# A mixture-of-experts stage that gathers its rows with two interleaved streams of indirect DMAs instead of blocks of eight

## The chip, the core and the metric

The kernel runs on one core of a Trainium2 chip. A core has five engines with instruction streams of their own: PE (matrix products), DVE (vector work), ACT (activation functions, copies), POOL (general work; here it also begins the gathers) and SP (begins plain DMAs). They meet through semaphores only. Sixteen DMA engines carry out the transfers that the engines begin. The metric is the device time of one launch in microseconds (us); 2831.47 us is the median of three runs of the kernel before.

## What is computed

Two layers of a hybrid decoder trunk, for 256 prompt tokens and 64 sample tokens together (320 tokens in three tiles of 128, 128 and 64). In each layer two recurrences are followed by a "PEER" mixer and by a gated per-layer embedding. The change lies in the PEER mixer, in which every token takes, for each of 8 heads, the 16 best of 16,384 experts, each a row `u` and a row `v` of 1,024 floats:

```python
sv, si = lax.top_k(s, PEER_TOPK)
cand = sv[:, :, 0, :, None] + sv[:, :, 1, None, :]
cv, ci = lax.top_k(cand.reshape(...), PEER_TOPK)
idx = jnp.take_along_axis(cand_idx.reshape(...), ci, axis=-1)
gate = jax.nn.softmax(cv, axis=-1)
u = jnp.take(u_tab, idx, axis=0)
hid = jax.nn.gelu(jnp.einsum('td,thkd->thk', xb, u).astype(jnp.float32), approximate=False)
vv = jnp.take(v_tab, idx, axis=0)
return jnp.einsum('thk,thkd->td', (gate * hid).astype(xb.dtype), vv)
```

Every sum over `k` needs all of `u` and `v` from HBM: 16 x 2 rows of 4 KB a token and head.

## The kernel before, in words

The mixer of a layer is a loop of 20 steps (NSTEP): 8 heads for the first tile of tokens, 8 for the second, 4 for the sample tile (which holds its 64 tokens twice, so two heads go in one step). A step has two halves of eight experts (G = 8). One gather brings one expert's row for each of 128 tokens, 128 rows of 4 KB, into one slot of a ring of eight: `urow` for U and `vrow` for V, both in the large tile `arena` (so the profile calls them arena). A layer has 320 U and 320 V gathers. The engines share a step as follows:

- POOL begins the gathers (`gather_step`, U at L671, V at L677), in one order written in its loop. Ahead of a U gather it waits for `u_free`, which DVE raises when its dot product has used the row eight before; ahead of a V gather for `v_free`, which PE raises when it has used the V row eight before. At the start of a step it also waits for `idx_ready`, the expert numbers of the step.
- DVE (`dots`, L1179) forms the product of each landed U row with the tokens, eight to a half. After the first half of a step it picks the experts of the next step (`pick_experts`, L1108 to L1170), a chain of some 25 small instructions. After the second half comes, in some steps, part of the embedding (`embed`, L1203 and L1205).
- ACT (`weights`) takes gelu of the eight products (L1003) and, after DVE has multiplied by the gates, makes eight diagonal matrices of the weights (L1009), which need all eight products of the half.
- PE (`add_rows`) multiplies each diagonal matrix with its V row and sums in PSUM. Between the halves of steps 0 to 7 it forms the queries and scores of heads to come (`between`), with weights that SP loads.

The embedding of a finished tile of tokens is worked into later steps, by the table `behind`: tile 0 is normed after step 8, and its four column blocks (i, m) = (0, 0) to (0, 3) come after the second halves of steps 9, 10, 11 and 12; tile 1 is normed in step 16, its blocks come two after step 16 and two after step 17. In each of them PE does its matrix products after its `add_rows` of that half (L1997 to L2003 and behind), ACT takes a sigmoid (L1034), and DVE waits for that sigmoid (L1203), adds the result to `h`, and only then goes on to the dots of the next step. Tile 2 is done at the end.

Of the kernel before, what the change touches and what calls it, by code (L numbers as in the profile page):

```python
# [33 lines left out]
TOPK = 16  # L34
G = 8
# [5 lines left out]
def hybrid_trunk(nc, x_prompt, x_sample, state_gla, state_gdn, state_conv, p_prompt, p_sample,  # L41
# [28 lines left out]
    NSTEP = sum(STEPS)  # L70
# [12 lines left out]
    with ctx:  # L83
        def sb(name, shape, dt=F32):
            return ctx.enter_context(nc.sbuf_tensor(name, shape, dt))
# [40 lines left out]
        idx_u = sb("idx_u", [P, 2, TOPK], U32)  # L126
# [22 lines left out]
        def view(off, *dims, rows=P):  # L149
            n = 1  # L150
            for d in dims:
                n *= d
            assert off + n <= ARENA, (off, dims)
            v = arena[0:rows, off:off + n]
            if len(dims) == 2:
                v = v.rearrange("p (a b) -> p a b", b=dims[1])
            elif len(dims) == 3:
                v = v.rearrange("p (a b c) -> p a b c", b=dims[1], c=dims[2])
            return v
# [77 lines left out]
        urow = view(0, G, D)  # L237
        vrow = view(G * D, G, D)
# [57 lines left out]
        def lsem(name):  # L296
            layer_sems.append(sem(name))
            return layer_sems[-1]
# [111 lines left out]
        idx_ready = lsem("idx_ready")  # L410
        u_loaded = [lsem(f"u_loaded{r}") for r in range(G)]
        v_loaded = [lsem(f"v_loaded{r}") for r in range(G)]
        u_free = lsem("u_free")
        v_free = lsem("v_free")
# [120 lines left out]
        def _(pool):  # L535
# [41 lines left out]
            with pool.Fori(0, DEPTH) as layer:  # L577
# [81 lines left out]
                u_l = peer_u.rearrange("l e d -> (l e) d")  # L659
                v_l = peer_v.rearrange("l e d -> (l e) d")  # L660

                def gather_step(step):

                        par_ = step % 2
                        pool.wait_ge(idx_ready, step + 1)
                        for half in range(2):
                            done = step * TOPK + half * G
                            for r in range(G):
                                at = idx_u[:, par_, half * G + r:half * G + r + 1]
                                pool.wait_ge(u_free, done + r + 1)  # L670
                                pool.indirect_dma_start(  # L671
                                    urow[:, r, :], None, u_l,
                                    bass.IndirectOffsetOnAxis(ap=at, axis=0)).then_inc(u_loaded[r], 16)
                            for r in range(G):
                                at = idx_u[:, par_, half * G + r:half * G + r + 1]
                                pool.wait_ge(v_free, done + r + 1)
                                pool.indirect_dma_start(  # L677
                                    vrow[:, r, :], None, v_l,
                                    bass.IndirectOffsetOnAxis(ap=at, axis=0)).then_inc(v_loaded[r], 16)

                for step in range(NSTEP):
                    gather_step(step)

                pool.wait_ge(u_free, G + NSTEP * TOPK)
                pool.wait_ge(v_free, G + NSTEP * TOPK)
# [30 lines left out]
        def _(act):  # L716
# [46 lines left out]
            with act.Fori(0, DEPTH) as layer:  # L763
# [135 lines left out]
                for k, (to, _, _, who) in enumerate(solve):  # L899
                    for i in solve_tiles(k):  # L900
                        n += 1
                        if who == "act":
                            R = ROWS[i]
                            act.wait_ge(solve_mm, n)
                            act.activation(slot(to[i], R)[:, :, 0:R], heads(i + 3 * (k % 2), R, R),
                                           ACT.Copy).then_inc(solve_act, 1)
# [153 lines left out]
        def _(dve):  # L1060
# [146 lines left out]
            with dve.Fori(0, DEPTH) as layer:  # L1207
# [215 lines left out]
                for k, (to, _, _, who) in enumerate(solve):  # L1423
                    for i in solve_tiles(k):
                        n += 1
                        R = ROWS[i]
                        src, t = heads(i + 3 * (k % 2), R, R), slot(to[i], R)[:, :, 0:R]
                        if who == "act":
                            continue
                        dve.wait_ge(solve_mm, n)  # L1430
                        if k == N_T:
                            own.after(dve.scalar_tensor_tensor(
                                slot(SH[i])[:, :, :], src, -1.0, over_heads(ident, R), ALU.mult,
                                ALU.add))
                        if who == "+":
                            dve.tensor_tensor(t, src, t, ALU.add).then_inc(solve_dve, 1)
                        else:
                            dve.tensor_copy(t, src).then_inc(solve_dve, 1)
# [633 lines left out]
```

## Time and profile before

| | us |
|---|---|
| three runs | 2816.63, 2837.72, 2831.47 (median 2831.47) |
| the profiled execution's own time | 2820.99 |
| its span | 2819.5 |
| PE / DVE / POOL busy in the span | 2185.9 / 1435.8 / 1548.5 |
| first dot to last dot of the mixer, layer 1 | 366.1 to 1357.9 |
| first dot to last dot of the mixer, layer 2 | 1761.0 to 2757.9 |

The two mixers take about 1,990 of the 2,820 us. The profile tells for each engine what it did when, and for an idle stretch what ended it. A gather shows twice: as an instruction of POOL, which is the time that POOL takes to begin it, and in the DMA share, which is how busy the sixteen DMA engines were. It has landed some time after POOL's instruction ended. "<-issue" behind an idle time says that the engine waited for nothing that the profile shows; "<-remote" that a semaphore ended the wait whose writer the profile doesn't name.

### The profile page before, as it was taken

What the parts mean: (1) busy time and instruction counts of PE and PEld (TensorE: products, weight loads), DVE (VectorE), ACT (ScalarE), POOL (GpSimd) and SP (SyncE); (2) the same over time, 40 slices, a digit from 0 to 9 for tenths busy, and PEclk for the clock granted to TensorE, in tenths of its full rate; (3) what the DMA queues carried; (4) which work ended last, traced back from release to release, by engine and by line L of the source; (5) the groups of instructions that cost most, each with busy time, mean ns of one, the idle gap of its engine ahead of it and who ended that gap; (6) DMA issues with size and microseconds to landing.
All of it is one profiled execution on the core that took longest, in us unless ns stands there. A gap on an engine that the chain in (4) does not pass through costs nothing.

```text
span 2819.5 us, 22006 instructions
## 1 busy us (share of the span) xinstructions
PE 2185.9 (78%) x6992; PEld 1231.9 (44%) x6992; DVE 1435.8 (51%) x3577; ACT 655.5 (23%) x1520; POOL 1548.5 (55%) x1385
## 2 busy tenths in 40 slices
PE   7999888877858576767799888898886667764775
PEld 5658654433323232334366676544432233332343
DVE  1446355565654565555224553565665556566452
ACT  3232222221221121221231431221221212112212
POOL 1113076777766677766210131767676766777661
PEclk9988999998878788889899999999987887897897
DMA  6310299999998889988463104999999988899783
GB/s 189 120 58 8 79 347 361 365 383 381 353 358 314 296 308 341 359 289 320 161 183 113 50 5 144 368 359 386 356 384 360 327 303 309 302 366 344 279 322 124
DMA packets 258740, 759.32 MB, mean 269 GB/s; under 512 B 26908, under 2 KB 89300, under 8 KB 258620
## 3 DMA queue, kind: packets, MB, share of 16 engines
q0 software_dynamic: 188480, 686.97, 65.7%
q1 hardware_dynamic: 70140, 70.88, 7.8%
q8 instruction: 60, 0.98, 0.1%
q14 instruction: 60, 0.49, 0.1%
HBM read 749.04 MB, written 8.72 MB: 269 GB/s over the span
## 4 chain that ended last, share of the span: by engine, by line
PE 40%; DVE 18%; issue 14%; POOL 12%; another core or an unknown queue 7%; ACT 5%; DMA 4%; SPq 0%; DVEq 0%; ACTq 0%; POOLq 0%; PEldq 0%
PE ps L1519 39%; DVE arena L1179 9%; POOL arena L671 6%; POOL arena L677 6%; DMA arena<-in_peer_u_dram,idx_u 2%; DMA arena<-in_peer_v_dram,idx_u 1%; ACT arena L1009 1%; DMA wring<-in_w_peer_q_dram 1%; ACT L1003 1%; DVE pick L1159 0%; DVE arena L1149 0%; DVE ci L1141 0%; PE ps L1535 0%; DVE arena L1155 0%
## 5 line engine op out<-in xcount | busy, mean ns | idle before, releaser
L1519 PE MATMUL ps<-arena 128*128 128x512 f32 (+5 forms) x3736 | 1427.3, 542 | 510.1 <-ACT arena L1009 386.1
L1519 PEld LDWEIGHTS ps<-arena 128*128 128x128 f32 (+3 forms) x3736 | 675.5, 206 | 1243.1 <-issue 1202.0
L677 POOL DMA_INDIRECT arena<-in_peer_v_dram,idx_u x640 | 755.2, 1180 | 313.2 <-issue 179.3
L671 POOL DMA_INDIRECT arena<-in_peer_u_dram,idx_u x640 | 687.8, 1075 | 335.2 <-issue 190.7
L1179 DVE CUSTOM_DVE_ANT_0 arena<-arena,xn 128x1024 f32<-128x1024 f32 x640 | 755.4, 1221 | 224.3 <-DMA arena<-in_peer_u_dram,idx_u 199.4
L1519 PE MATMUL ps<-aT,wring 128*128 128x320 f32 (+2 forms) x1344 | 362.9, 430 | 20.7 <-DMA wring<-in_w_peer_q_dram 11.2
L1519 PEld LDWEIGHTS ps<-aT,wring 128*128 128x128 f32 x1344 | 253.3, 196 | 129.7 <-issue 25.9
L1519 PE MATMUL ps<-wring,aT 128*128 128x256 f32 (+1 forms) x960 | 222.7, 388 | 5.8 <-ACT aT L1024 4.5
L1519 PEld LDWEIGHTS ps<-wring,aT 128*128 128x128 f32 (+1 forms) x960 | 177.3, 189 | 52.3 <-issue 20.8
L1203 DVE TENSOR_TENSOR arena<-arena,ps 128x256 f32<-128x256 f32 x24 | 10.1, 421 | 336.9 <-ACT arena L1034 336.9
L1003 ACT ACTIVATE gelu<-hid 128x8 f32<-128x8 f32 x80 | 16.6, 208 | 642.7 <-DVE hid L1179 440.0
L1009 ACT ACTIVATE arena<-ident,wgt 128x128 f32<-128x128 f32 x512 | 157.0, 388 | 20.8 <-DVE wgt L1185 11.5
L598 POOL TENSOR_TENSOR arena<-arena 128x1024 f32<-128x1024 f32 x4 | 12.3, 3106 | 216.1 <-PE ps L1519 109.9
L1185 DVE TENSOR_TENSOR wgt<-gelu,gate 128x8 f32<-128x8 f32 x80 | 13.4, 168 | 183.9 <-ACT gelu L1003 114.0
L1034 ACT ACTIVATE arena<-ps 128x256 f32<-128x256 f32 x24 | 9.2, 384 | 279.9 <-remote 185.0
L1003 ACT ACT_TABLE_LOAD x54 | 69.3, 1283 | 0.9
L588 POOL TENSOR_TENSOR arena<-xn,seqmask 64x1024 f32<-64x1024 f32 x8 | 16.1, 2033 | 94.0 <-ACT xn L789 94.0
L973 ACT ACTIVATE arena<-ps 128x320 f32<-128x320 f32 (+1 forms) x32 | 13.6, 424 | 228.5 <-PE ps L1519 212.5
L982 ACT ACTIVATE arena<-ps 128x256 f32<-128x256 f32 x30 | 10.0, 381 | 212.9 <-PE ps L1519 97.4
L933 ACT ACT_TABLE_LOAD x40 | 51.3, 1283 | 4.8 <-issue 4.1
L1179 DVE DVE_READ_ACCUMULATOR2_ANT hid<- 128x1 f32 x640 | 52.0, 81 | 0.0
L639 POOL TENSOR_TENSOR arena<-arena,seqmask 64x1024 f32<-64x1024 f32 x8 | 14.9, 1890 | 62.3 <-ACT arena L915 62.3
(293 smaller groups left out, 1460.6 us busy)
## 6 DMA issues: line engine op xcount, KB each, us to landing
wring<-in_w_in_dram SPq DMA_DIRECT2D x28, 1024.0 KB
wring<-in_w_peer_q_dram SPq DMA_DIRECT2D x16, 1024.0 KB
arena<-in_peer_u_dram,idx_u POOLq DMA_INDIRECT x640
arena<-in_peer_v_dram,idx_u POOLq DMA_INDIRECT x640
wring<-in_w_out_dram SPq DMA_DIRECT2D x8, 1024.0 KB
wring<-in_w_ple_gate_dram SPq DMA_DIRECT2D x8, 1024.0 KB
arena<-in_state_gdn_dram POOLq DMA_DIRECT2D x2, 2048.0 KB, 15.4
out_dram<-arena POOLq DMA_DIRECT2D x2, 2048.0 KB, 11.7
```

Of the source, the lines that this page charges most:

```text
L588: ins = pool.tensor_tensor(vmask[:, hd, :, :], v1[0:64, 2, hd * P:(hd + 1) * P].unsqueeze(1).to_broadcast([64, NB, P]), seqmask[:, :].unsq ...
L598: ins = pool.tensor_tensor(s_, s_, d.to_broadcast([P, NB, P]), ALU.mult)
L639: ins = pool.tensor_tensor(dvm[hd], vnew(2, 64)[:, hd, :].unsqueeze(1).to_broadcast([64, NB, P]), seqmask[:, :].unsqueeze(2).to_broadcast( ...
L671: pool.indirect_dma_start(urow[:, r, :], None, u_l, bass.IndirectOffsetOnAxis(ap=at, axis=0)).then_inc(u_loaded[r], 16)
L677: pool.indirect_dma_start(vrow[:, r, :], None, v_l, bass.IndirectOffsetOnAxis(ap=at, axis=0)).then_inc(v_loaded[r], 16)
L933: act.activation(gexp[:, :], cv[:, :], ACT.Exp, bias=ncv[:, 0:1], accum_out=esum[:, 0:1]).then_inc(gate_exp, 1)
L973: act.activation(qT[:, c, t0:NT], ps[:, 6 + c, t0:NT], ACT.Copy)
L1003: act.activation(gelu[:, par_, c], hid[:, par_, c], ACT.Gelu).then_inc(gelu_ready, 1)
L1009: act.activation(diag[:, r, :], unit[:, :], ACT.Copy, scale=wgt[:, par_, k:k + 1]).then_inc(diag_ready, 1)
L1179: dve.tensor_tensor_reduce(out=urow[:, r, :], in0=urow[:, r, :], in1=xn[:, tile, :], scale=1.0, scalar=0.0, op0=ALU.mult, op1=ALU.add, acc ...
L1185: dve.tensor_tensor(wgt[:, par_, c], gelu[:, par_, c], gate[:, par_, c], ALU.mult).then_inc(wgt_ready, 1)
L1519: return pe.matmul(out, lhsT, rhs, start=start, stop=stop, skip_group_check=True)
```

## The change

In the old loop POOL begins the gathers of a half as eight U and then eight V, then the next half. In the new one a counter k runs over all U rows of the layer; at each k the U gather of row k is begun, and then the V gather of row k - 8. So the V rows of a half are begun one by one between the U rows of the half after it. The waits ahead of each gather keep their semaphores and counts, and the wait for `idx_ready` stands ahead of the first U row of a step. DVE, ACT, PE and SP keep their orders, instruction for instruction.

```diff
                 u_l = peer_u.rearrange("l e d -> (l e) d")
                 v_l = peer_v.rearrange("l e d -> (l e) d")
 
-                def gather_step(step):
-
-                        par_ = step % 2
+                def gather_u(k):
+                    step, c, r = k // TOPK, k % TOPK, k % G
+                    if c == 0:
                         pool.wait_ge(idx_ready, step + 1)
-                        for half in range(2):
-                            done = step * TOPK + half * G
-                            for r in range(G):
-                                at = idx_u[:, par_, half * G + r:half * G + r + 1]
-                                pool.wait_ge(u_free, done + r + 1)
-                                pool.indirect_dma_start(
-                                    urow[:, r, :], None, u_l,
-                                    bass.IndirectOffsetOnAxis(ap=at, axis=0)).then_inc(u_loaded[r], 16)
-                            for r in range(G):
-                                at = idx_u[:, par_, half * G + r:half * G + r + 1]
-                                pool.wait_ge(v_free, done + r + 1)
-                                pool.indirect_dma_start(
-                                    vrow[:, r, :], None, v_l,
-                                    bass.IndirectOffsetOnAxis(ap=at, axis=0)).then_inc(v_loaded[r], 16)
-
-                for step in range(NSTEP):
-                    gather_step(step)
+                    at = idx_u[:, step % 2, c:c + 1]
+                    pool.wait_ge(u_free, k + 1)
+                    pool.indirect_dma_start(
+                        urow[:, r, :], None, u_l,
+                        bass.IndirectOffsetOnAxis(ap=at, axis=0)).then_inc(u_loaded[r], 16)
+
+                def gather_v(k):
+                    step, c, r = k // TOPK, k % TOPK, k % G
+                    at = idx_u[:, step % 2, c:c + 1]
+                    pool.wait_ge(v_free, k + 1)
+                    pool.indirect_dma_start(
+                        vrow[:, r, :], None, v_l,
+                        bass.IndirectOffsetOnAxis(ap=at, axis=0)).then_inc(v_loaded[r], 16)
+
+                for k in range(NSTEP * TOPK + G):
+                    if k < NSTEP * TOPK:
+                        gather_u(k)
+                    if k >= G:
+                        gather_v(k - G)
 
                 pool.wait_ge(u_free, G + NSTEP * TOPK)
                 pool.wait_ge(v_free, G + NSTEP * TOPK)
```

POOL's order at the start of a layer's mixer, before. L671 is a U gather and L677 a V gather, x8 means eight in a row, and the waits are in brackets; the last two rows begin the second step:

```order
L671 DMA arena<-in_peer_u_dram,idx_u 128x1024 [waits u_free] x7
L677 DMA arena<-in_peer_v_dram,idx_u 128x1024 [waits v_free] x8
L671 DMA arena<-in_peer_u_dram,idx_u 128x1024 [waits u_free] x8
L677 DMA arena<-in_peer_v_dram,idx_u 128x1024 [waits v_free] x8
L671 DMA arena<-in_peer_u_dram,idx_u 128x1024 [waits u_free,idx_ready]
L671 DMA arena<-in_peer_u_dram,idx_u 128x1024 [waits u_free] x7
```

The same place now, up to the fourth V gather; L668 is U and L676 is V. The alternation goes on so through all 20 steps:

```order
L668 DMA arena<-in_peer_u_dram,idx_u 128x1024 [waits u_free] x8
L676 DMA arena<-in_peer_v_dram,idx_u 128x1024 [waits v_free]
L668 DMA arena<-in_peer_u_dram,idx_u 128x1024 [waits u_free]
L676 DMA arena<-in_peer_v_dram,idx_u 128x1024 [waits v_free]
L668 DMA arena<-in_peer_u_dram,idx_u 128x1024 [waits u_free]
L676 DMA arena<-in_peer_v_dram,idx_u 128x1024 [waits v_free]
```

The ninth U gather, which needs the first dot, has moved ahead of the first V gather; before, all eight V gathers stood ahead of it.

The end of a layer's mixer on POOL, before:

```order
L671 DMA arena<-in_peer_u_dram,idx_u 128x1024 x8
L677 DMA arena<-in_peer_v_dram,idx_u 128x1024 x8
L671 DMA arena<-in_peer_u_dram,idx_u 128x1024 x8
L677 DMA arena<-in_peer_v_dram,idx_u 128x1024 x8
```

and now:

```order
L668 DMA arena<-in_peer_u_dram,idx_u 128x1024
L676 DMA arena<-in_peer_v_dram,idx_u 128x1024
L668 DMA arena<-in_peer_u_dram,idx_u 128x1024
L676 DMA arena<-in_peer_v_dram,idx_u 128x1024
L668 DMA arena<-in_peer_u_dram,idx_u 128x1024
L676 DMA arena<-in_peer_v_dram,idx_u 128x1024 x9
```

Between the last eight U gathers there now stand V gathers of the half before, and nine V gathers close the layer instead of eight.

## Rows read from the trace of the kernel before

**Rows 1.** The page's costliest groups: line, engine, count | busy, mean ns | idle before.

```profile
L677 POOL DMA_INDIRECT arena<-in_peer_v_dram,idx_u x640 | 755.2, 1180 | 313.2 <-issue 179.3
L671 POOL DMA_INDIRECT arena<-in_peer_u_dram,idx_u x640 | 687.8, 1075 | 335.2 <-issue 190.7
...
L1203 DVE TENSOR_TENSOR arena<-arena,ps 128x256 f32<-128x256 f32 x24 | 10.1, 421 | 336.9 <-ACT arena L1034 336.9
```

**Rows 2.** Busy time by stretch: PE, PEld, DVE, ACT, POOL; PEclk, DMA share, GB/s.

```profile
366.00:753.00 387.00, 321.25 (x865) 163.92 (x866) 225.86 (x578) 84.47 (x234) 289.40 (x253) 0.92 0.97 369
753.00:868.00 115.00, 79.09 (x175) 35.44 (x173) 59.29 (x149) 24.77 (x60) 74.49 (x75) 0.81 0.93 355
868.00:1033.00 165.00, 113.08 (x258) 53.07 (x258) 85.85 (x225) 34.12 (x76) 114.55 (x96) 0.82 0.85 305
1033.00:1290.00 257.00, 177.15 (x416) 83.00 (x416) 145.30 (x372) 52.57 (x131) 180.57 (x160) 0.83 0.89 327
2265.00:2428.00 163.00, 112.45 (x258) 52.94 (x258) 85.16 (x222) 33.38 (x76) 113.06 (x96) 0.82 0.86 309
2428.00:2690.00 262.00, 174.63 (x416) 82.34 (x416) 146.10 (x374) 53.33 (x131) 180.60 (x160) 0.84 0.88 321
```

**Rows 3.** Timeline of POOL in step 12: start, us, instruction, idle time before it.

```profile
983.96 1.99 POOL L671 DMA_INDIRECT arena<-in_peer_u_dram,idx_u  x1 [0.31 <-issue]
...
993.52 0.94 POOL L677 DMA_INDIRECT arena<-in_peer_v_dram,idx_u  x1 [0.30 <-issue]
...
1007.61 0.94 POOL L677 DMA_INDIRECT arena<-in_peer_v_dram,idx_u  x1 [0.30 <-issue]
1008.85 0.94 POOL L671 DMA_INDIRECT arena<-in_peer_u_dram,idx_u  x1 [0.30 <-issue]
...
1027.54 0.94 POOL L677 DMA_INDIRECT arena<-in_peer_v_dram,idx_u  x1 [0.30 <-issue]
```

**Rows 4.** Timeline of PE, ACT and DVE in step 12 and after it.

```profile
1007.51 15.67 PE L1519 MATMUL ps<-arena 128*128 128x512 f32 x32 [2.30 <-ACT arena L1009]
1023.02 1.03 PE L1519 MATMUL ps<-arena,pT 128*128 128x256 f32 x4
...
1024.60 3.72 PE L1519 MATMUL ps<-wring,aT 128*128 128x256 f32 x16
...
987.47 0.21 ACT L1003 ACTIVATE gelu<-hid 128x8 f32<-128x8 f32 x1 [8.81 <-DVE hid L1179]
...
1006.53 0.21 ACT L1003 ACTIVATE gelu<-hid 128x8 f32<-128x8 f32 x1 [10.98 <-DVE hid L1179]
...
1031.78 0.38 ACT L1034 ACTIVATE arena<-ps 128x256 f32<-128x256 f32 x1 [21.07 <-remote]
...
1032.20 0.42 DVE L1203 TENSOR_TENSOR arena<-arena,ps 128x256 f32<-128x256 f32 x1 [25.26 <-ACT arena L1034]
...
1033.00 1.22 DVE L1179 CUSTOM_DVE_ANT_0 arena<-arena,xn 128x1024 f32<-128x1024 f32 x1
...
1034.14 1.22 DVE L1179 CUSTOM_DVE_ANT_0 arena<-arena,xn 128x1024 f32<-128x1024 f32 x1
```

**Rows 5.** POOL's waits over the span: us in total, times, longest.

```profile
POOL arena L671 <- DVE hid L1179: 82.9, 12, 11.8
POOL arena L677 <- PE ps L1519: 82.5, 89, 5.4
```

**Rows 6.** Timeline of PE in steps 3 and 4: where two adds begin.

```profile
512.35 17.00 PE L1519 MATMUL ps<-arena 128*128 128x512 f32 x44 [2.89 <-ACT arena L1009]
...
556.93 17.01 PE L1519 MATMUL ps<-arena 128*128 128x512 f32 x44 [2.89 <-ACT arena L1009]
```

**Rows 7.** The chain that ended last: a gather on it, start and us.

```profile
1163.22 6.24 DMA arena<-in_peer_u_dram,idx_u
```

**Rows 8.** Timeline of POOL at the end of the second mixer.

```profile
2764.05 0.94 POOL L677 DMA_INDIRECT arena<-in_peer_v_dram,idx_u  x1 [0.30 <-issue]
```

**Rows 9.** Timeline of DVE in the pick of step 14.

```profile
1092.94 0.43 DVE L1138 MAX8 cv<-arena 128x8 f32<-128x256 f32 x1 [5.34 <-issue]
```

## The prediction, made before the changed kernel ran

> **What bounds the kernel now.** I read the costliest groups of the page first. The two gather lines of Pool, 640 instructions each, are busy 755 and 688 us of the 2819.5 us, and one row shows a different loss: DVE stands idle 336.9 us ahead of only 24 instructions of L1203, the adding of the embedding [rows 1]. The busy table by stretch then cuts the first layer's mixer stage by steps: steps 0 to 7, 8 and 9, 10 to 12, 13 to 17 [rows 2]. In steps 0 to 7 Pool starts 253 gathers in 387 us, one in 1.53 us, with the DMA engines at a share of 0.97. In steps 10 to 12 it starts 96 in 165 us, 55 us a step, with the DMA share at 0.85; the second layer's stretch (163 us) repeats it. So there are two regimes.
>
> In the first, Pool's issue and the transfers run at about the same pace. A gather is busy 0.94 us and the next follows after 0.30 us, 1.24 us in all, while some take 1.99 us, and these stand where DVE runs its dots (1.22 us each, one every 1.14 us) [rows 3, 4]. The mean busy time in steps 0 to 7 is 289.40 / 253 = 1.144 us, so without any wait an issue would cost 1.144 + 0.30 = 1.444 us and a step of 32 issues 46.2 us [rows 2]. The rest up to 1.53 us is waiting: Pool waited 82.5 us ahead of V gathers until PE had used a row, and 82.9 us ahead of U gathers for dots [rows 5]. PE is close behind: its adding of V rows came round after 44.6 us (512.35 to 556.93) [rows 6].
>
> In the second regime, the steps that end with an embed, the chain is another. In step 12 the first V gather of the second half starts at 993.52, the last at 1007.61; then Pool runs on by itself and starts the next step's eight U and eight V gathers, 1008.85 to 1027.54, while DVE waits 25.26 us in L1203 [rows 3, 4]. That wait ends with PE's eight rows (15.67 us from 1007.51), PE's embed (1023.02 to 1024.60 + 3.72 = 1028.3), ACT's sigmoid at 1031.78 and DVE's add; the next dots start at 1033.00. So the second regime is a chain of DVE, PE and ACT, and half of Pool's issues lie beside it for nothing.
>
> **The change, part by part.** No gather is added or removed: 1,280 issues, 671 MB, the same two rings of eight rows. The waits are the same in number. What moves: U of a half now goes ahead of V of the half before, one by one. A U gather needs the dot of the row eight before it; the V gather behind it in Pool's order now waits with it. Before, the eight V gathers of the half stood ahead of these U gathers and could start while DVE was in its pick of experts or in an embed.
>
> *Steps with an embed (10 to 12).* While DVE waits in L1203 no dot ends, so Pool stands at the first U gather of the next half, and there is nothing to start: the V rows of the half that is waited for are the last that it may issue. The 16 issues at 1008.85 to 1027.54 that were free come into the chain. From a step's first dot to the next step's: dot 1.3; 31 issues ahead of the last V gather at 1.24 = 38.4; two bursts of dots, each with four issues of 1.99 instead of 0.94, 8 x 1.05 = 8.4; landing 6.0 (the chain shows 6.24 from issue to landing [rows 7]); the last row on PE 15.67 / 8 = 2.0; embed 5.3; sigmoid and two adds 0.38 + 0.42 + 0.42 = 1.2. Sum 62.6 against 55.0, so 3 x 7.6 = +23 us a layer. DVE's own work is covered: a burst of dots takes 8 x 1.14 = 9.2 us, and from one burst's gelu to the next's are 1006.53 - 987.47 = 19.1 us [rows 4], so the pick between them takes 9.9. Both end 19 us after the first dot, before Pool has issued the 16 gathers that come first, so Pool doesn't wait for the pick there. Bounds: four long issues instead of eight and a landing of 5 give 57.4; the lag between PE's end (1028.3) and the sigmoid (1031.78), which I leave out because the transfers will have run dry by then, gives 66.1 if it stays.
>
> The landing is the one term on which a page speaks. The Trainium skill, "DMA: Bandwidth & Descriptors", section "Anatomy of one DMA", fits 2.0 us + bytes / 436e3, an estimate of 3.2 us for 512 KB; the trace's 6.24 differs and decides. By the page each such cycle would be 2.8 us shorter, 22 us over the eight of both layers.
>
> *Steps 0 to 9.* From step 0's first dot to step 10's lie 387 + 115 = 502 us [rows 2]. In the new order Pool issues 20 halves of 16 in between; the last begins after 319 issues, and 1.3 + 6.0 + 2.0 + 5.3 + 1.2 = 15.8 us stand around them. At 1.444 us an issue that is 476 us, at the present 1.53 us 504 us. The V waits of eight-row blocks should shrink, since a V row is asked for some 22 us after its predecessor landed. But PE's and ACT's loop of 44.6 us, SP's weight blocks, and a new wait remain: U gathers need the first dot after a pick, which by 32 x 1.444 = 46 us a step comes only some 5 us before Pool's turn. I take 1.49 us: 491 us, -11.
>
> *Steps 13 to 17.* Before: 257 us, and 262 us in the second layer [rows 2]. New: step 13 starts with all rows landed; the last V gather of step 16 begins after 1.3 + 127 x 1.444 = 184.7; landing, row, two embeds (10.6) and the adds make 204.5; step 17 with its two embeds takes 62.6 + 5.3 = 67.9. Sum 272.4, +15, and +10 in the second layer; mean +12.5. Here the 16 gathers that were prefetched beside the embed are paid back, so no gain is counted for them.
>
> *Tail.* Step 18 of the second layer begins where the stretch from 2428 ends, at 2690, and the last V gather starts at 2764.05, 74 us later [rows 2, 8]. New: 1.3 + 55 x 1.444 = 80.7, +6.5.
>
> Sum a layer: -11 + 23 + 12.5 + 6.5 = +31; two layers +62. Against the profiled execution's 2820.99 us that is **2883 us**; the median of the three runs shown is 2831.47, 10 us above it, inside what the runs differ by, so I leave the sum there.
>
> **The rivals.** *Faster: the V waits go and nothing else counts.* Pool never waits in steps 0 to 9 (1.444 us, -26), the embed cycles cost their lower bound (+2.4 each: +7 for steps 10 to 12, and 272.4 - 10.4 = 262, +3 to +5 for 13 to 17), and the tail costs nothing: -26 + 7 + 4 = -15 a layer, 2791 us. For it speak the 82.5 us of V waits [rows 5]; against it, that all 32 issues of an embed step, at 1.24 us or more, now lie inside its chain. It decides when the mean issue falls below 1.45 us in steps 0 to 9. Chance 0.12.
>
> *Flat.* Steps 0 to 9 gain 20 us a layer and embeds cost half of my price: about 2830 us. Chance 0.25.
>
> *Worse: more issues meet a dot.* Dots now run one by one as U rows land, every two issues, instead of in bursts of eight; each may hold up the issue beside it. At present (1.144 - 0.94) / 1.05 x 32 = 6 of 32 issues are long [rows 2, 3]. If ten are, a step costs 4.2 us more, over the 28 steps without an embed +118: 3001 us. The same sign has a pick that stands idle between its steps, as 5.34 us ahead of one MAX8 in step 14 [rows 9], once it outlasts the 5 us of slack. Against: isolated dots meet at most one issue, and an overlap shorter than a burst needn't hold it. Chance 0.13.
> The Trainium skill, "SBUF — State Buffer", section "SBUF: two separate sides", gives that rival a rule: a DVE operation with two SBUF inputs and a GpSimd one that reads SBUF exclude each other for a whole instruction. The 1.99 us issues beside dots agree with it; no run here yet shows dots one by one.
>
> *Not what it says.* Pool has one instruction order, written in the loop, so the order itself can't fail to change.
>
> **How the numbers follow.** My forecast (2845 to 2945) has 0.50, flat 0.25, faster 0.12, worse 0.13. The bounds of the terms give 2807 (1.444 us, 57.4 us cycles) to 2965 (1.53 us, 66.1 us cycles); with the rivals' ends cut to two in ten the range is 2815 to 2960. A change of 1%, 28 us, is about what a measurement of this kernel can tell from none. Above 2849: most of the forecast and the worse rival, 0.62; within 1%: 0.26; below 2793: 0.12.
>
> **What would show it.** Right: the steps with an embed are about 62 us long, Pool's wait ahead of U gathers for dots grows from 83 us to some 150 or more, waits ahead of V for PE nearly vanish, and the DMA share falls below 0.8 in steps 10 to 12. The last V gather of a half starts some 14 us or less before DVE's next dots. Wrong: embed steps at 55 us or below, or steps 0 to 7 faster than 1.45 us an issue; then Pool's waits, not its issue, were the price. If the mean gather is busy over 1.25 us, the worse rival holds.

## The result, and the profile of the changed kernel

The changed kernel takes 3076.16 us (median of 4 runs, 3054.41 to 3080.42), the kernel before 2834.59 us in the same rounds: a ratio of 1.085, 95% interval 1.079 to 1.091. I had forecast 2883 us and a range up to 2960. The direction was right and the size was not: the loss is 242 us where I worked out 62. The profiled execution took 3072.53 us and its span is 3071.0 us, 251.5 more than before.

The costliest groups of the page after, which answer to [rows 1] (L668 is the U gather, L676 the V gather, L1205 the embed's add, L1181 the dots; columns as there):

```profile
L668 POOL DMA_INDIRECT arena<-in_peer_u_dram,idx_u x640 | 714.0, 1116 | 672.5 <-DVE hid L1181 425.6
L1181 DVE CUSTOM_DVE_ANT_0 arena<-arena,xn 128x1024 f32<-128x1024 f32 x640 | 755.7, 1223 | 387.0 <-DMA arena<-in_peer_u_dram,idx_u 377.9
L676 POOL DMA_INDIRECT arena<-in_peer_v_dram,idx_u x640 | 758.2, 1185 | 200.0 <-issue 166.4
L1205 DVE TENSOR_TENSOR arena<-arena,ps 128x256 f32<-128x256 f32 x24 | 10.1, 421 | 392.7 <-ACT arena L1036 392.7
```

Busy on the gathers is 714.0 + 758.2 = 1472 us against 1443 before, only 29 us more. What grew is the idle time ahead of U gathers, 335 to 673 us, and the releaser that ends most of it is now the dot of DVE. POOL's waits of after say the same, against [rows 5] (us in total, times, longest):

```profile
POOL arena L668 <- DVE hid L1181: 425.6, 35, 20.8
POOL arena L676 <- PE ps L1521: 33.0, 97, 3.7
```

So the waits for PE fell from 82.5 to 33.0 us, as the order promised, and those for dots rose from 82.9 to 425.6 us. Waiting changed places, and much more came than went.

Where in the program? Busy time by stretch in layer 1 of after: steps 0 to 9, 10 to 12, 13 to 17 (us, then PE, PEld, DVE, ACT, POOL, granted clock, DMA share, GB/s, as in [rows 2]):

```profile
364.00:934.00 570.00, 420.98 (x1038) 192.87 (x1038) 282.56 (x726) 109.11 (x294) 361.21 (x320) 0.92 0.84 315
934.00:1122.00 188.00, 115.63 (x258) 46.31 (x258) 86.48 (x225) 34.38 (x76) 112.95 (x96) 0.91 0.73 268
1122.00:1414.00 292.00, 190.34 (x416) 74.88 (x416) 145.41 (x372) 53.06 (x131) 183.17 (x160) 0.91 0.78 288
```

The DMA share fell in each (steps 0 to 7 had 0.97 before), and the granted clock of TensorE is 0.91 to 0.92 throughout, no lower than in any stretch of [rows 2], so the clock is no part of the loss. The differences by stage, from first dot to first dot, beside the terms of the sum:

| stretch | before, layer 1 / 2 | after, layer 1 / 2 | change | forecast |
|---|---|---|---|---|
| steps 0 to 9 | 502.3 / 504.3 | 570.3 / 562.3 | +68 / +58 | -11 |
| steps 10 to 12 | 164.5 / 163.3 | 187.4 / 187.9 | +23 / +25 | +23 |
| steps 13 to 17 | 257.3 / 261.5 | 292.1 / 286.4 | +35 / +25 | +15 / +10 |
| steps 18, 19, to the last dot | 66.5 / 66.6 | 76.9 / 75.2 | +10 / +9 | +6.5 (to the last V gather) |

Of the 190 us that the forecast missed, 148 lie in steps 0 to 9 (79 + 69). They are the question of the experiments.

The steps with an embed came as forecast. Timeline of POOL, then PE, ACT and DVE, in step 12 of after, whose first dot ran at 1058.77; it answers to [rows 3, 4]:

```profile
1106.98 0.94 POOL L676 DMA_INDIRECT arena<-in_peer_v_dram,idx_u  x1 [0.31 <-issue]
1123.38 1.69 POOL L668 DMA_INDIRECT arena<-in_peer_u_dram,idx_u  x1 [15.46 <-DVE hid L1181]
...
1113.51 1.98 PE L1521 MATMUL ps<-arena 128*128 128x512 f32 x4 [0.50 <-DMA arena<-in_peer_v_dram,idx_u]
...
1116.92 3.72 PE L1521 MATMUL ps<-wring,aT 128*128 128x256 f32 x16
...
1120.67 0.38 ACT L1036 ACTIVATE arena<-ps 128x256 f32<-128x256 f32 x1 [24.26 <-PE ps L1521]
...
1121.09 0.42 DVE L1205 TENSOR_TENSOR arena<-arena,ps 128x256 f32<-128x256 f32 x1 [28.45 <-ACT arena L1036]
...
1121.89 1.22 DVE L1181 CUSTOM_DVE_ANT_0 arena<-arena,xn 128x1024 f32<-128x1024 f32 x1
```

After its last V gather POOL does nothing for 15.46 us; PE gets that row, the embed follows, the sigmoid, the add, and only the next dot lets POOL go on. First dot to first dot is 63.1 us (forecast 62.6), the last V gather starts 48.2 us behind the first dot (48.1) and the next dots 14.9 us behind that (14.5). The sigmoid came 0.03 us after PE's end (1116.92 + 3.72), not 3.5 us as in [rows 4].

### The profile page after: what moved, and what is told of

Its sections match the earlier page's. It is cut to its first block, busy times and chain, and to the rows that moved or that the text cites. A ratio compares the mean times of both kernels' runs of the same rounds, so it can differ in the third digit from the quotient of the medians.

```text
span 3071.0 us, 22006 instructions
## 1 busy us (share of the span) xinstructions
PE 2262.7 (74%) x6992; PEld 1184.7 (39%) x6992; DVE 1432.3 (47%) x3577; ACT 656.1 (21%) x1520; POOL 1578.0 (51%) x1385
## 4 chain that ended last, share of the span: by engine, by line
PE 32%; POOL 23%; issue 13%; DVE 13%; DMA 12%; another core or an unknown queue 4%; ACT 3%; SPq 0%; DVEq 0%; ACTq 0%; POOLq 0%; PEldq 0%
PE ps L1521 31%; POOL arena L668 11%; POOL arena L676 11%; DMA arena<-in_peer_v_dram,idx_u 8%; DVE arena L1181 4%; DMA arena<-in_peer_u_dram,idx_u 2%; DMA wring<-in_w_peer_q_dram 1%; ACT arena L1011 0%; DVE cv L1140 0%; DVE pick L1161 0%; DVE arena L1151 0%; DVE arena L1157 0%; DVE topi L1130 0%; DVE arena L1119 0%
## 5 line engine op out<-in xcount | busy, mean ns | idle before, releaser
L1521 PE MATMUL ps<-arena 128*128 128x512 f32 (+5 forms) x3736 | 1506.5, 545 | 695.4 <-DMA arena<-in_peer_v_dram,idx_u 320.1
L1521 PEld LDWEIGHTS ps<-arena 128*128 128x128 f32 (+3 forms) x3736 | 629.3, 202 | 1553.5 <-issue 797.8
L668 POOL DMA_INDIRECT arena<-in_peer_u_dram,idx_u x640 | 714.0, 1116 | 672.5 <-DVE hid L1181 425.6
L1181 DVE CUSTOM_DVE_ANT_0 arena<-arena,xn 128x1024 f32<-128x1024 f32 x640 | 755.7, 1223 | 387.0 <-DMA arena<-in_peer_u_dram,idx_u 377.9
L676 POOL DMA_INDIRECT arena<-in_peer_v_dram,idx_u x640 | 758.2, 1185 | 200.0 <-issue 166.4
L1205 DVE TENSOR_TENSOR arena<-arena,ps 128x256 f32<-128x256 f32 x24 | 10.1, 421 | 392.7 <-ACT arena L1036 392.7
L598 POOL TENSOR_TENSOR arena<-arena 128x1024 f32<-128x1024 f32 x4 | 12.7, 3193 | 212.5 <-DVE arena L1330 212.5
L1187 DVE TENSOR_TENSOR wgt<-gelu,gate 128x8 f32<-128x8 f32 x80 | 13.5, 169 | 224.4 <-ACT gelu L1005 139.7
L984 ACT ACTIVATE arena<-ps 128x256 f32<-128x256 f32 x30 | 10.0, 381 | 292.2 <-remote 153.3
L1181 DVE DVE_READ_ACCUMULATOR2_ANT hid<- 128x1 f32 x640 | 53.0, 83 | 0.0
L935 ACT ACTIVATE gexp<-cv,ncv 128x16 f32<-128x16 f32 x40 | 12.3, 307 | 188.7 <-DVE ci L1143 138.5
```

The lines of the kernel that those rows point to most:

```text
L598: ins = pool.tensor_tensor(s_, s_, d.to_broadcast([P, NB, P]), ALU.mult)
L668: pool.indirect_dma_start(urow[:, r, :], None, u_l, bass.IndirectOffsetOnAxis(ap=at, axis=0)).then_inc(u_loaded[r], 16)
L676: pool.indirect_dma_start(vrow[:, r, :], None, v_l, bass.IndirectOffsetOnAxis(ap=at, axis=0)).then_inc(v_loaded[r], 16)
L935: act.activation(gexp[:, :], cv[:, :], ACT.Exp, bias=ncv[:, 0:1], accum_out=esum[:, 0:1]).then_inc(gate_exp, 1)
L1181: dve.tensor_tensor_reduce(out=urow[:, r, :], in0=urow[:, r, :], in1=xn[:, tile, :], scale=1.0, scalar=0.0, op0=ALU.mult, op1=ALU.add, acc ...
L1187: dve.tensor_tensor(wgt[:, par_, c], gelu[:, par_, c], gate[:, par_, c], ALU.mult).then_inc(wgt_ready, 1)
```

## The experiments

Two theories stood against each other. A: V gathers queue behind U gathers that want a dot, so every stop of DVE (embed, pick, wait for gelu) now stops both streams. B: gathers run beside single dots more often, and each such issue is long. Of the 1,280 issues 242 lasted over 1.5 us after and 212 before, 6.05 and 5.3 of 32, which already spoke against B; other orders of the same gathers put both to a number.

**Four other orders of the same gathers.** `e1_block8` keeps the lag of eight rows but begins U and V in blocks of eight, so that no V gather stands between two U gathers of a half:

```diff
-                for k in range(NSTEP * TOPK + G):
-                    if k < NSTEP * TOPK:
-                        gather_u(k)
-                    if k >= G:
-                        gather_v(k - G)
+                for h in range(2 * NSTEP + 1):
+                    for k in range(h * G, h * G + G):
+                        if h < 2 * NSTEP:
+                            gather_u(k)
+                    for k in range(h * G - G, h * G):
+                        if h > 0:
+                            gather_v(k)
```

> V stays one half behind U, as in the changed kernel, but in blocks: eight U gathers of the next half, then eight V gathers of this half. Theory A (the half that V stands behind U: V rows wait behind U gathers that need the dots after a pick or an embed): as slow as the changed kernel or slower, 3050 to 3130 us, embed steps 60 us or more, Pool's wait ahead of U for dots over 400 us. Theory B (the alternation as such: dots one by one, tables in turn, more long issues): back at about 2835 us.

Measured: 3220.53 us, ratio 1.140 [1.132, 1.147]. B falls: with blocks of eight again, as before the change, the kernel is not back at 2830 us but slower still. By A, the V block now stands behind all eight dots ahead of it instead of behind one at a time; A's figure was too low by 90 us.

`e2_lag4` and `e4_lag0` put V four rows and no row behind U:

```diff
-                for k in range(NSTEP * TOPK + G):
+                LAG = 4
+                for k in range(NSTEP * TOPK + LAG):
                     if k < NSTEP * TOPK:
                         gather_u(k)
-                    if k >= G:
-                        gather_v(k - G)
+                    if k >= LAG:
+                        gather_v(k - LAG)
```

> The alternation stays, V runs four rows behind U instead of eight. Theory A: four of the eight V rows of a half no longer stand behind the next half's U, so embed steps go to about 55 us and steps 0 to 9 to 48 to 50 us each: 2800 to 2880 us in all, Pool's wait ahead of U for dots about half of 426 us. Theory B: about 3075 us, since the alternation is the same.

> The alternation with no lag: V of a row right behind U of the same row. Theory A in its general form (in one Pool order every gather waits for the slowest wait ahead of it): now U rows stand behind V gathers that need PE's rows of the half before, so U can't be fetched ahead during dots; about 54 to 56 us a plain step, 3000 to 3100 us, and Pool's waits move from U for dots to V for PE. Theory B: about 3075 us with waits as in the changed kernel.

Measured: 2917.44 us for four rows (1.033 [1.027, 1.039]) and 3343.63 us for none (1.183 [1.175, 1.191]); A's windows were missed above by 37 and 244 us, its order held. `e3_instep` alternates only within a step: all V gathers of a step are begun before the first U gather of the next:

```diff
+                for step in range(NSTEP):
+                    k0 = step * TOPK
+                    for k in range(k0, k0 + G):
+                        gather_u(k)
+                    for k in range(k0 + G, k0 + TOPK):
+                        gather_u(k)
+                        gather_v(k - G)
+                    for k in range(k0 + G, k0 + TOPK):
+                        gather_v(k)
```

> V runs eight rows behind U inside a step only: U 0 to 7, then U 8 to 15 in turn with V 0 to 7, then V 8 to 15 as a block before the next step begins. No V row stands behind a U gather of the next step any more. Theory A: the embed chain has 24 issues instead of 32 (62.6 - 8 x 1.24 = 52.7 us, below the 55 us of DVE, PE and ACT), and Pool goes on through a pick: 2800 to 2860 us. Theory B: half of the gathers still alternate, so about 2950 us.

Measured: 2889.03 us, 1.020 [1.015, 1.026], 29 us above the window. Now POOL's waits of the four, in the order e1, e2, e4, e3 (us, times, longest):

```profile
POOL arena L668 <- DVE hid L1183: 526.7, 40, 29.9
...
POOL arena L676 <- PE ps L1523: 38.4, 31, 4.0
```

```profile
POOL arena L668 <- DVE hid L1182: 204.6, 29, 14.7
...
POOL arena L676 <- PE ps L1522: 81.5, 85, 13.0
```

```profile
POOL arena L676 <- PE ps L1522: 734.1, 171, 11.6
...
POOL arena L668 <- DVE hid L1182: 69.9, 13, 7.2
```

```profile
POOL arena L668 <- DVE hid L1185: 165.9, 15, 24.6
...
POOL arena L676 <- PE ps L1525: 92.7, 75, 9.0
```

The two waits together are 165 us before, 259 in e3, 286 in e2, 459 in the changed kernel, 565 in e1 and 804 in e4, and the times rise in that order. The lag decides which of two things a V gather queues behind: at no lag its own slot, which PE frees only after the whole half's weights (734 us); at eight rows the dot that the U gather ahead of it wants. TensorE's granted clock was lower in e1 and e4 (0.84 and 0.83 over the run, 0.92 in the changed kernel), but PE was not busy longer for it: 418.6 and 410.8 us in steps 0 to 9 of the first layer, against 421.0. e3 is instructive for steps 10 to 12:

```profile
865.00:1032.00 167.00, 113.38 (x258) 49.71 (x258) 85.98 (x223) 33.99 (x76) 113.51 (x96) 0.87 0.83 302
1032.00:1311.00 279.00, 187.85 (x416) 82.16 (x416) 146.40 (x374) 53.65 (x131) 183.25 (x160) 0.84 0.82 301
```

In these windows of e3 (columns as in [rows 2]) the embed steps cost 167 us as before; from step 0 to step 12 its first layer took 667.6 us against 666.8, and its second 682.2 against 667.5; the changed kernel took 757.7 and 750.2. With no V gather of a step left behind the U gathers of the next, the loss of the first 13 steps is gone in one layer and down to 15 us in the other, alternation and all. It loses later, 279 against 257 us in steps 13 to 17. There step 13 took 46.8 us against 36.7, since only the eight U rows and no V rows are begun during an embed; steps 16 and 17 took 136.9 against 124.2, which was not followed up.

**Taking away DVE's stops.** If A holds, the changed order should lose less where DVE stops less. The first edit moves the embed's last part, ACT's sigmoid and DVE's add, from the end of a step to behind the pick in the next step; PE's part stays:

```diff
+        late = {s_ + 1: behind[s_, 1] for s_ in (HP + 1, HP + 2, HP + 3, HP + 4, 2 * HP, 2 * HP + 1)}
...
                         pick_experts(step + 1, (step + 1) % 2)
+                    for i, m in late.get(step, ()):
+                        embed(i, m, own)
...
                     for i, m in behind.get((step, 1), ()):
-                        embed(i, m, own)
+                        if step + 1 not in late:
+                            embed(i, m, own)
```

(and the same in ACT's loop, behind `softmax`). The second edit leaves out DVE's pick in all steps but the first of a layer, and keeps its semaphores:

```diff
             def pick_experts(step, par_):
+                if step > 0:
+                    own = Steps(dve, pick_step)
+                    dve.max_index(ci[:, 8:16], cv[:, 8:16], cand2[:, :]).then_inc(cv_ready, 1)
+                    dve.wait_ge(gate_exp, step + 1)
...
+                    dve.tensor_scalar(idx_u[:, par_, :], idx_f[:, :], table_base[:, 0:1], None,
+                                      ALU.add).then_inc(idx_ready, 1)
+                    dve.sem_clear(pick_step)
+                    return
```

Each was run on the changed order and on the old one, alone and together, so that the gap between the two orders can be read with and without each stop. The four kernels without a pick compute something else: every step gathers the rows of step 0 again. So they are compared with each other. Of the pick itself 5.0 us are left in most steps of e7 and e8, where 1.5 had been expected.

> The changed kernel, with the wait for the embed taken off DVE's way: ACT's sigmoid and DVE's add of the six embeds behind steps 9 to 12, 16 and 17 are done one half later (ACT behind the weights of the next step's first half, DVE behind the pick that follows). All work stays. Theory A: the two things that hold dots back are the embed and the pick with its gelu wait; without the first, steps 10 to 12 fall from 62.6 to about 50 us and 16 and 17 likewise, 2900 to 2960 us. Rival C (the embed steps only show a loss that Pool or the DMA engines would set anyway): no change, 3060 to 3080 us.

> The same shift of the embed in the kernel before. Its embed chain is 55 us of DVE, PE and ACT with Pool running on beside it. Theory A: steps 10 to 12 go to the 47 us of a plain step, about -8 us for each of 12 embed steps: 2730 to 2770 us. Rival C: the steps are Pool's or the DMA engines' and stay at 2835 us.

> The changed kernel with the pick of experts left out in all steps but the first (about 1.5 us of it stay; every step uses the experts of step 0, so the time is that of the same gathers with a shorter stop of DVE). Theory A: Pool's wait ahead of U gathers in steps 0 to 9 is a wait for the first dot behind the pick, so these steps lose 8 to 12 us each, from 57 to about 47 us: 2850 to 2920 us. Rival D (the loss in steps 0 to 9 comes from the V rows that reach PE late, through queries and scores, whatever DVE does): at most 40 us less, 3030 us or more.

> The kernel before with the same pick left out. Its Pool does not wait for the dots behind a pick, since eight V gathers stand there to be begun. Theory A: little, 2770 to 2830 us, so that the gap to the changed kernel falls from 241 to about 100 us, which is that of the embed steps and the tails. Rival D: the gap stays above 180 us.

> The changed kernel with both stops of DVE taken away: the embed one half later, and the pick of experts left out in all steps but the first (every step uses the experts of step 0). Theory A (the loss is DVE's two stops, which the new order makes Pool's stops): the gap to the same edits of the kernel before closes to less than 60 us, 2710 to 2760 us. Rival E (a part of the loss of 80 us or more has nothing to do with these stops: gathers one by one, PE waiting for single V rows): 2790 us or more.

> The kernel before with the same two edits, as the measure for the run beside it: about 2735 less the 36 us that the pick alone was worth, 2680 to 2720 us.

| | old order | new order | gap |
|---|---|---|---|
| as it is | 2834.59 | 3076.16 | 242 |
| embed late (e6, e5) | 2734.66, ratio 0.973 [0.966, 0.980] | 2899.76, ratio 1.032 [1.026, 1.037] | 165 |
| no pick (e8, e7) | 2772.31, ratio 0.987 [0.981, 0.992] | 2913.86, ratio 1.037 [1.032, 1.042] | 142 |
| both (e10, e9) | 2718.37, ratio 0.963 [0.958, 0.969] | 2779.71, ratio 0.985 [0.979, 0.991] | 61 |

(Ratios are to the kernel before in the same rounds.) e5 to e8 and e10 lie in the windows of A, e5 at its lower edge (but the gap that is left without a pick, 142 us, had been expected at about 100); e9 lies 20 us above A's and 10 us below that of its rival, so between the two. The late embed takes 77 us of the gap, the missing pick 100, both together 180: nearly additive, and three quarters of the whole. In steps 0 to 9, the place of the miss, the pick is nearly all of it. The windows of e7 and then of e8 over them:

```profile
367.00:870.00 503.00, 406.40 (x1038) 192.90 (x1037) 202.54 (x396) 109.68 (x294) 372.48 (x320) 0.94 0.95 356
```

```profile
369.00:869.00 500.00, 400.03 (x1038) 199.08 (x1038) 208.52 (x396) 109.51 (x294) 343.69 (x327) 0.90 0.97 367
```

Without a pick the two orders take 503 and 500 us there, with it 570 and 502 (in the second layer 499 and 497, with it 562 and 504). That the rows of step 0 come again and again doesn't explain it: the old order with the same edit moves 367 GB/s there at a DMA share of 0.97 (369 and 0.97 in steps 0 to 7 before), and is only 2 and 8 us shorter. The new order's DMA share is back at 0.95. Its POOL is 29 us busier than the old one's, for seven issues fewer (66 of them over 1.5 us against 29: theory B's long issues), and that does not lengthen the stretch. POOL's wait for dots over the same steps of the changed kernel (the window of its steps 0 to 9 above):

```profile
POOL arena L668 <- DVE hid L1181: 103.1, 10, 18.3
```

Nine of the ten waits, 99 us, are for the first dot behind a pick, in every step but step 7. The kernel before has none there; e7 has three, 20.1 us together. And over the whole of e7 and of e9:

```profile
POOL arena L668 <- DVE hid L1193: 254.4, 19, 21.0
```

```profile
POOL arena L670 <- DVE hid L1198: 119.8, 16, 14.1
```

They go from 425.6 to 254.4 and 119.8 us as the stops of DVE go; with the late embed alone they are 262.4.

Why the last 61 us remain isn't settled; where they lie can be read. From step 18 to the last dot e9 takes 97.0 us a layer (97.2 and 96.8) and e10 78.9, so 36 us for both layers; steps 10 to 12 add 18 and steps 13 to 17 add 19; in steps 0 to 9 e9 is 14 us ahead. The late embed still holds DVE in both, 186 us in e9 and 150 in e10, so it parts them by 36 us at most. e9 also has 218 long issues against 116 in e10, which is 102 x 1.05 = 107 us of POOL; how much of that lies on the path, no run tells.

**Can the orders be combined?** `e11_instep_late` is e3 with the late embed, `e12_lag4_late` is e2 with it; the edits are those shown.

> V eight rows behind U inside a step only, and the embed one half later; nothing is left out. Theory A: no V row stands behind a dot that waits for an embed or for the next step; if the V waits of Pool in the kernel before (110 us of them with the late embed) go too, 2690 to 2730 us, else the 2735 us of the late embed alone.

> V four rows behind U throughout, and the embed one half later. Theory A: between the late embed with eight rows of lag (2900 us) and with the old order (2735 us), 2770 to 2830 us, as four of eight V rows still stand behind the dots after a pick.

Measured: 2758.24 us (0.979 [0.972, 0.985]) and 2818.51 us (0.994 [0.989, 0.999]). e12 lies in its window; e11 lies above every figure expected of it, 24 us above the old order with the late embed; but the two ran in different rounds, and their ratios, 0.979 and 0.973, have intervals that overlap, so which is faster isn't shown. Both gain much from that edit, and neither is shown to beat e6. The fastest kernel measured that computes everything is `e6_before_late`, 2734.66 us, 0.973 of the kernel before: the old order of gathers, with the embed's add moved half a step. Its steps 10 to 12 take 143.7 us in the first layer, against 164.5.

## Why the prediction was right in one part and wrong in another

**Right: the mechanism and the embed steps.** "the V gather behind it in Pool's order now waits with it" is what happened, and where DVE stops for an embed the sum holds: 62.0, 62.3 and 63.1 us for steps 10 to 12 (62.6 forecast), 67.2 and 67.9 us for step 17 (67.9). It holds term by term: the steps 10 to 12 of both layers and step 17 have seven or eight issues over 1.5 us each, eight had been put in. The DMA share of 0.73 there and waits for dots above 150 us were named. That the waits for PE "nearly vanish" was too much: 33.0 of 82.5 us are left.

**Wrong: the term for steps 0 to 9, "I take 1.49 us: 491 us, -11".** It rests on the sentence that the first dot after a pick "comes only some 5 us before Pool's turn". That slack was not there: in the first layer POOL waits for that dot in nine of the ten steps, 11 us in the mean. Timeline of POOL, DVE and ACT of after in steps 3 and 4; the dots at 569.79 and 624.14 are the first of the second halves:

```profile
571.78 1.18 POOL L668 DMA_INDIRECT arena<-in_peer_u_dram,idx_u  x1 [9.96 <-DVE hid L1181]
...
593.61 0.94 POOL L668 DMA_INDIRECT arena<-in_peer_u_dram,idx_u  x1 [0.30 <-issue]
...
616.01 0.94 POOL L676 DMA_INDIRECT arena<-in_peer_v_dram,idx_u  x1 [0.31 <-issue]
...
569.79 1.22 DVE L1181 CUSTOM_DVE_ANT_0 arena<-arena,xn 128x1024 f32<-128x1024 f32 x1
...
602.48 1.22 DVE L1181 CUSTOM_DVE_ANT_0 arena<-arena,xn 128x1024 f32<-128x1024 f32 x1 [1.71 <-DMA arena<-in_peer_u_dram,idx_u]
...
608.54 0.21 DVE L1187 TENSOR_TENSOR wgt<-gelu,gate 128x8 f32<-128x8 f32 x1 [4.83 <-issue]
...
614.98 0.09 DVE L1136 MATCH_VALUE_LOAD arena<-cv,arena 128x8 f32 x1 [2.26 <-remote]
...
619.90 0.43 DVE L1140 MAX8 cv<-arena 128x8 f32<-128x256 f32 x1 [3.98 <-remote]
...
624.14 1.22 DVE L1181 CUSTOM_DVE_ANT_0 arena<-arena,xn 128x1024 f32<-128x1024 f32 x1
...
607.22 0.66 ACT L984 ACTIVATE arena<-ps 128x256 f32<-128x256 f32 x2 [19.42 <-PE ps L1521]
...
608.30 0.21 ACT L1005 ACTIVATE gelu<-hid 128x8 f32<-128x8 f32 x1
```

POOL is done with its 32 issues at 616.95, 45.2 us after its start, so the cost of an issue was right; it then waits for the dot that starts at 624.14. From 569.79 to there lie 54.3 us. By the prediction's own terms it would be 1.3 + 14 x 1.444 + 6.0 + 1.1 = 28.6 us until the first half's last dot has ended, and 9.9 for the pick: 38.5 us, and POOL's turn would come after 1.3 + 32 x 1.444 = 47.5 us. (That is a slack of some 8 us when the dot's own 1.2 us are taken off, not 5.) Three things came on top:

- The dots of the first half end at 603.63, 33.8 us after 569.79, 5.2 more. The last U gather starts at 593.61 and its dot at 602.48, 8.9 us later, where 6.0 had been taken for the landing, which is 2.9 of the 5.2; the rest is POOL's later start and four long issues among the 14. The 6.24 of [rows 7] was read behind a stretch with a DMA share of 0.71 (1150 to 1160 of before); here it is 1.03 (593 to 603, 417 GB/s). That the load made the difference is likely, not shown.
- DVE then waits 4.9 us for the first half's gelu. ACT gives it only after its copies of the scores (L984), and these wait for PE, which adds V rows first, and V rows come a half later now. I had costed this wait at nothing without saying so. It was there before too, and was harmless there: POOL waited for no dot in steps 0 to 9, having eight V gathers to begin that needed none.
- The pick lasts 15.6 us instead of 9.9, with DVE idle ahead of single small instructions (2.26 and 3.98 us). The 9.9 came from step 12, one of the short picks; those of steps 0 to 9 average 12.4 us before and 13.5 after, over both layers.

5.2 + 4.9 + 5.7 and 38.5 make the 54.3. The step is a usual one: steps 2 to 8 of this layer take 48.0 to 59.3 us, 54.2 in the mean. Over steps 0 to 9 of the first layer DVE's waits (the first four of after, then those of before; us, times, longest) show the first two; the L1187 rows put down to "issue" are waits for gelu as well, since each ends 0.03 us behind a gelu's end:

```profile
DVE arena L1181 <- DMA arena<-in_peer_u_dram,idx_u: 100.9, 53, 5.2
DVE wgt L1187 <- ACT gelu L1005: 61.1, 13, 20.2
DVE wgt L1187 <- issue: 42.3, 7, 9.5
DVE arena L1205 <- ACT arena L1036: 28.4, 1, 28.4
```

```profile
DVE arena L1179 <- DMA arena<-in_peer_u_dram,idx_u: 63.2, 37, 9.5
DVE wgt L1185 <- ACT gelu L1003: 45.6, 12, 8.6
DVE wgt L1185 <- issue: 35.3, 8, 12.8
```

The gelu wait went from 80.9 to 103.4 us, the wait for U rows from 63.2 to 100.9. It is a ring: a late dot makes V rows late, PE's scores come late behind them, gelu and the pick behind those, and the next dot. That the pick is the link that closes it is shown by e7 against e8. The wait for gelu alone does not do it: in e7 it is longer still, 154.8 us over these steps, and the loss is gone. How much of the loss belongs to each of the three was read from one step's timeline and not tested by itself.

**The worse rival.** It named the right second clause, a pick "once it outlasts the 5 us of slack", and gave it no price, while its priced mechanism, ten long issues of 32, did not come: the mean gather is busy (714.0 + 758.2) / 1280 = 1.150 us, below the 1.25 us that I had set, and e1, with no alternation, was slower still. The rule of the Trainium skill, "SBUF — State Buffer", section "SBUF: two separate sides", that I had put beside it is borne out by this trace as to which issues are long: of the 1,280 issues of after 456 begin while a dot runs, and 350 of these last over 1.0 us; of the 824 others 31 do. The prediction's "needn't hold it", of overlaps shorter than a burst, was wrong. What failed is the rival's own premise that dots one by one meet more issues: 432 had begun inside a dot before the change. The rule does not decide the time here: POOL's busy time above 0.94 us an issue went from 240 to 269 us, and 29 us more is all that the long issues can have cost.

**Steps 13 to 17 and the tail.** +35 and +25 for +15 and +10: step 17 was right, so the rest is in steps 13 to 16. It is the same error: their term, "1.3 + 127 x 1.444 = 184.7" to the last V gather of step 16, has no wait of POOL in it. Measured are 204.8 and 198.7 us, with POOL waiting for dots behind a pick 9.9 us in step 14 and 10.5 in step 16 of the first layer, and 8.4 in step 15 of the second: that is all of the 20 us in the one layer and 8.4 of the 14 in the other. In step 16 the norm of tile 1 (L1195 to L1199, 4.9 us of DVE) lies between pick and dots as well. From that gather to step 17's first dot are 20.2 and 19.8 us, where 19.8 had been added. e7 does not take these stops away: it still takes 285 and 273 us in steps 13 to 17, 39 and 26 more than e8, and in its step 16 DVE still waits 19.9 and 10.1 us where the pick was, for ACT's exponentials, ahead of that norm. (In the faster rival, 262 us against 257 and 262 is +5 and 0, not "+3 to +5"; its 2791 us would be 3 us lower at most.) In the tail the last V gather starts 83.0 us behind step 18's first dot against 73.9, +9 for the +6.5 forecast.

## What to carry to other kernels

When one engine begins two streams in order, a gather that waits holds up every gather behind it: put behind a wait only what must wait, and let the stream that has free slots go ahead where the consumer of the other stops. A wait that shows in the profile as harmless is harmless by what covers it; before moving that cover, add up the whole path from release to release under the load that it will run in, with durations read in that same regime. And look at the stop itself: moving the add that DVE waited in by half a step gained 2.7% with the old order, while every other order of the gathers that was tried without it cost time.

## What the runs showed of the chip

DVE's pick, the same chain of some 25 small instructions in every step, has no fixed length. From the instruction that ends the wait for gelu (L1185) to the pick's last, 19 of 38 picks before and 18 of 38 after take 9.4 to 9.7 us. The others take up to 25.9 us, and the means are 12.7 and 12.6. All picks of steps 10 to 13 and 17, where about 290 to 320 GB/s move, are of the short kind, in both kernels; among those where the DMA share is near 1 both kinds are found, and in the changed kernel six of the long ones ran at shares of 0.70 to 0.82. Of step 14 before, whose pick runs from 1080.4 to 1104.1, two rows of DVE's timeline beside that of [rows 9], and then the window over it (columns as in [rows 2]):

```profile
1096.45 0.17 DVE L1143 TENSOR_SCALAR cij<-ci 128x16 uint32<-128x16 uint32 x1 [2.30 <-remote]
...
1099.95 0.18 DVE L1147 CAST cijf<-cij 128x32 f32<-128x32 uint32 x1 [3.25 <-remote]
```

```profile
1080.00:1104.00 24.00, 13.97 (x32) 6.00 (x32) 8.85 (x41) 5.62 (x13) 15.31 (x17) 0.91 0.99 404
```

The instructions keep their lengths; DVE stands between them, 5.34, 2.30 and 3.25 us at a time, each time ahead of an instruction that by the kernel's code waits for a count raised by an instruction of the pick before it, and here in a stretch in which the transfers have no slack (share 0.99). Whether the transfers cause it or only run at the same time, no run here tells: none held the transfers back with everything else the same.

An issue of a gather that begins while a dot runs waits that dot out. In the changed kernel 347 issues began with 0.2 to 1.2 us of a dot still to run; every one of them ended 0.81 to 0.83 us behind that dot's end, whatever was left of it, and so did all 288 of the kernel before. Where the issue began first and a dot began within its 0.94 us, the issue was not lengthened: 2 of 198 lasted over 1.0 us. So what an issue loses to a dot, about 1.05 us at most, depends on which of the two begins first.
